# Two transformer blocks on one core: the opening's vector loads, its scales and its order of turning rearranged

## The reference, cut to what matters

```python
h = jnp.concatenate([meta, x], axis=1)          # 16 meta tokens + 256 tokens, width 2048
u = rms_norm(h, norm_mix_pre[i])                # xf * rsqrt(mean(xf * xf) + eps) * g
u = conformer_conv(u, conv_w_in[j], ...)        # begins with u @ w_in + b_in, w_in 2048 x 4096
...                                             # layer norm, swiglu, then the second block with its experts
```

## Time and profile before

| | us |
|---|---|
| median of three timed runs (2286.61 to 2288.72) | 2287.68 |
| span of the profiled execution | 2283.6 |
| TensorE busy in it | 2254.0 |
| VectorE, ScalarE, GpSimd busy | 1607.3, 1208.3, 248.0 |

### The profile page before, as it was taken

The page is one execution under the profiler, slowest core; times in us unless marked ns, Lnnn a source line. Parts: engine busy times, 40 slices in busy tenths (PEclk is TensorE's granted clock), DMA queues, the critical chain, the costliest instruction groups (busy, mean ns, idle before and its releaser), DMA issues.

```text
span 2283.6 us, 34678 instructions
## 1 busy us (share of the span) xinstructions
PE 2254.0 (99%) x12099; PEld 1943.3 (85%) x12099; DVE 1607.3 (70%) x1910; ACT 1208.3 (53%) x1229; POOL 248.0 (11%) x107
## 2 busy tenths in 40 slices
PE   9999999999999999999999999999999999999997
PEld 8999788888888888888888888888887888888886
DVE  2999776565556554545587665567558898999997
ACT  4445456444444444344553454444356778787785
POOL 4898101000000000000100000000010000101000
PEclk9999999999999999999999999999999999999999
DMA  7665256776676665555577666655566999999995
GB/s 202 177 177 175 104 195 167 192 188 184 189 191 189 184 191 183 196 189 197 173 191 206 170 185 193 188 166 184 185 239 238 385 370 365 375 369 391 370 378 229
DMA packets 446150, 514.93 MB, mean 225 GB/s; under 512 B 12911, under 2 KB 407847, under 8 KB 410279
## 3 DMA queue, kind: packets, MB, share of 16 engines
q1 hardware_dynamic: 443268, 502.21, 67.6%
q0 software_dynamic: 2544, 11.66, 1.3%
q10 hardware_dynamic: 272, 0.20, 0.0%
HBM read 512.36 MB, written 6.29 MB: 227 GB/s over the span
## 4 chain that ended last, share of the span: by engine, by line
PE 92%; DVE 3%; issue 2%; ACT 2%; POOL 1%; DVEq 0%; ACTq 0%; POOLq 0%
PE ps L2438 25%; PE ps L2332 16%; PE ps L2443 13%; PE ps L2647 10%; PE ps L2664 7%; PE ps L2652 5%; PE ps L2512 2%; PE ps L2251 2%; PE ps L2233 2%; PE ps L2234 2%; ACT whi L726 1%; DVE ps L1385 1%; PE ps L2345 1%; POOL wlo L556 1%; PE ps L2174 1%
## 5 line engine op out<-in xcount | busy, mean ns | idle before, releaser
L726 ACT ACTIVATE whi<-raw 128x2048 fp32r<-128x2048 f32 x286 | 547.4, 1914 | 359.6 <-PE ps L2332 184.8
L1305 DVE TENSOR_TENSOR wlo<-raw,whi 128x2048 fp32r<-128x2048 f32 x248 | 567.8, 2289 | 205.4 <-ACT whi L726 205.4
L2438 PE MATMUL ps<-xT,whi 128*128 128x512 f32 x2656 | 638.9, 392 | 5.3 <-DVE xT L1749 4.3
L2438 PEld LDWEIGHTS ps<-xT,whi 128*128 128x128 f32 x2656 | 488.5, 189 | 99.8 <-issue 4.4
L2443 PEld LDWEIGHTS ps<-xT,wlo 128*128 128x128 f32 x2656 | 343.5, 192 | 14.3
L2443 PE MATMUL ps<-xT,wlo 128*128 128x256 f32 x2656 | 347.8, 283 | 0.0
L990 ACT ACTIVATE wk<-ps 128x256 f32<-128x256 f32 x184 | 68.8, 383 | 450.4 <-PE ps L2443 450.1
L2332 PE MATMUL ps<-whi,act 128*128 128x512 f32 x1088 | 259.5, 391 | 0.0
L2332 PEld LDWEIGHTS ps<-whi,act 128*128 128x128 f32 x1088 | 205.4, 189 | 43.6 <-ACT act L908 0.9
L1311 DVE TENSOR_TENSOR wlo<-raw,whi 128x2048 fp32r<-128x2048 f32 x94 | 214.2, 2288 | 3.9 <-ACT whi L736 3.5
L736 ACT ACTIVATE whi<-raw 128x2048 fp32r<-128x2048 f32 x88 | 168.1, 1914 | 32.2 <-PE ps L2647 23.1
(11 more groups left out here) (339 smaller groups left out, 2704.9 us busy)
## 6 DMA issues: line engine op xcount, KB each, us to landing
raw<-in_w_in SPq DMA_DIRECT2D x72, 1024.0 KB, 5.5
raw<-in_w_exp_up SPq DMA_DIRECT2D x56, 1024.0 KB, 7.4
raw<-in_ffn_w_gate SPq DMA_DIRECT2D x44, 1024.0 KB, 5.6
raw<-in_ffn_w_up SPq DMA_DIRECT2D x44, 1024.0 KB, 5.6
raw<-in_ffn_w_down SPq DMA_DIRECT2D x44, 1024.0 KB, 4.8
raw<-in_w_exp_gate SPq DMA_DIRECT2D x40, 1024.0 KB, 6.4
raw<-in_conv_w_in SPq DMA_DIRECT2D x32, 1024.0 KB, 6.0
more_raw<-in_w_exp_down SPq DMA_DIRECT2D x32, 1024.0 KB, 7.9
```

Source lines behind the costliest of these rows:

```text
L726: fn(whi[:, s % 2, :], raw[:, s % RING, :], ACT.Copy).then_inc(hi_ready, 1)
L1305: V.tensor_tensor(wlo[:, s % 2, :], raw[:, s % RING, :], whi[:, s % 2, :], ALU.subtract).then_inc(lo_ready, 1)
L2438: mm(ps[:, bank, :], whi[:, s % 2, at:at + P], xT5[:, k0 + k, :], start=(k == 0), stop=False)
```

## The change

The seven vector loads are issued by GpSimd in place of ScalarE. ScalarE squares and sums the meta tokens itself, takes their root, then square and root of token half 0, then of half 1, each root on its own; VectorE makes a reciprocal and a diagonal after each. TensorE multiplies ones 8 times, turns the meta tokens unscaled into bank 6 (16 transposes), multiplies ones 8 times, and makes a broadcast of the meta tokens' scales by a product of ones and `meta_d`. It turns half 0 for k = 0 to 7 as soon as its diagonal is there, two k to a bank, then the vectors, then half 1 for the same k. VectorE multiplies all turned meta tokens at once by the gain and by the scale (`metaF`), ScalarE copies them to `xTA` at k = 2, and VectorE makes their residue in one instruction. Evictions and residues take the 256 token columns alone. ScalarE makes the high part of panel 0 at k = 4 and of panel 1 at k = 8. TensorE's products begin at k = 12 of the turning, and after it k = 4 to 15 of panel 0 run with k = 0 to 7 of panel 1, followed by low products, the other eight k of panel 1 and its low products. In the diff, the declarations of six semaphores are left out.

```diff
--- before.py
+++ after.py
@@ -234,6 +234,7 @@
 
         x_d = tmp[:, 0, 0:T].rearrange("p (t c) -> p t c", t=TOK)
         meta_d = tmp[0:META, 0, T:T + META]
+        metaF = tmp[:, 0, 2 * T:2 * T + KT * META].rearrange("p (k c) -> p k c", k=KT)
 
         FIRST_ROWS, FIRST_TURN = (4, 5, 6, 7), (3, 1, 2, 4)
         OHG = TOK * (GROUPS + EXPERTS) + 2 + 2 * 4 * TOK
...
@@ -545,9 +552,14 @@
             pool.affine_select(out=ident[:, :], in_=ident[:, :], compare_op=ALU.not_equal, fill=1.0, base=0,
                                pattern=[[-1, P]], channel_multiplier=1).then_inc(ident_ready, 1)
 
+            for src, at in ((norm_mix_pre, V_PRE), (conv_b_in, V_BIN), (conv_b_dw, V_BDW), (conv_ln_g, V_LG),
+                            (conv_ln_b, V_LB), (norm_ffn_pre, V_FPRE), (norm_mix_g_2, V_MIX2)):
+                r = src.rearrange("a (k p) -> (a k) p", p=P)
+                pool.dma_start(vst[at:at + r.shape[0], 0, :], r).then_inc(vec_first, 16)
+
             pool.wait_ge(ssq_ready, 2)
             pool.memset(uext[:, :, 0:PAD], 0.0).then_inc(pad_ready, 1)
-            pool.wait_ge(meta_sq, 2)
+            pool.wait_ge(meta_sq, 1)
             pool.memset(sq_acc, 0.0).then_inc(acc_clear, 1)
 
             def panel_lo(g, s):
@@ -749,29 +761,35 @@
 
 
             a.dma_start(gB[0:META, :], meta_tokens).then_inc(meta_in, 16)
-            for src, at in ((norm_mix_pre, V_PRE), (conv_b_in, V_BIN), (conv_b_dw, V_BDW), (conv_ln_g, V_LG),
-                            (conv_ln_b, V_LB), (norm_ffn_pre, V_FPRE), (norm_mix_g_2, V_MIX2)):
-                r = src.rearrange("a (k p) -> (a k) p", p=P)
-                a.dma_start(vst[at:at + r.shape[0], 0, :], r).then_inc(vec_first, 16)
-
             a.wait_ge(var_ready, 3)
             warm(2)
-            for t in range(TOK):
-                a.wait_ge(x_in[t], 16)
-                squares(h[:, t, :], t)
+            a.wait_ge(meta_in, 16)
+            fn(tmp[0:META, 1, :], gB[0:META, :], ACT.Square, accum_out=st[0:META, SS + 2:SS + 3]).then_inc(meta_sq, 1)
+            a.wait_ge(meta_sq, 1)
+            fn(st[0:META, RT + 2:RT + 3], st[0:META, SS + 2:SS + 3], ACT.Sqrt, bias=st[0:META, EPS_AT:EPS_AT + 1],
+               scale=1.0 / D).then_inc(open_root, 1)
+            a.wait_ge(x_in[0], 16)
+            squares(h[:, 0, :], 0)
+            a.wait_ge(ssq_ready, 1)
+            fn(st[:, RT:RT + 1], st[:, SS:SS + 1], ACT.Sqrt, bias=st[:, EPS_AT:EPS_AT + 1],
+               scale=1.0 / D).then_inc(open_root, 1)
+            a.wait_ge(x_in[1], 16)
+            squares(h[:, 1, :], 1)
             a.wait_ge(ssq_ready, 2)
-            a.wait_ge(meta_sq, 2)
-            root(st[:, SS:SS + 3], st[:, RT:RT + 3], 1.0 / D, st[:, EPS_AT:EPS_AT + 1])
+            root(st[:, SS + 1:SS + 2], st[:, RT + 1:RT + 2], 1.0 / D, st[:, EPS_AT:EPS_AT + 1])
 
 
             a.wait_ge(vec_ready, 1)
             for k in range(KT):
                 if k == 2:
+                    a.wait_ge(meta_scaled, 2)
+                    fn(xTA[:, :, 0:META], metaF, ACT.Copy).then_inc(meta_hi, 1)
+                if k == 4:
                     hi(0, 0)
-                if k == 10:
+                if k == 8:
                     hi(0, 1)
-                a.wait_ge(turned, k + 1)
-                fn(xTA[:, k, 0:TM], ps[:, k % 4, 0:TM], ACT.Copy,
+                a.wait_ge(turned, k // 2 * 2 + 2)
+                fn(xTA[:, k, META:TM], ps[:, k // 2 % 4, k % 2 * T:k % 2 * T + T], ACT.Copy,
                    scale=vcol[:, V_PRE + k:V_PRE + k + 1]).then_inc(xhi_ready, 1)
 
 
@@ -1322,24 +1340,39 @@
             V.memset(st[:, EPS_AT:EPS_AT + 1], RMS_EPS).then_inc(var_ready, 1)
             V.memset(st[:, LN_EPS_AT:LN_EPS_AT + 1], LN_EPS).then_inc(var_ready, 1)
 
-            v.wait_ge(var_ready, 1)
-            v.wait_ge(meta_in, 16)
-            V.tensor_tensor(tmp[0:META, 1, :], gB[0:META, :], gB[0:META, :], ALU.mult).then_inc(meta_sq, 1)
-            v.wait_ge(meta_sq, 1)
-            V.reduce_sum(st[0:META, SS + 2:SS + 3], tmp[0:META, 1, :], AX_X).then_inc(meta_sq, 1)
+            v.wait_ge(ident_ready, 1)
+            v.wait_ge(open_root, 1)
+            V.reciprocal(st[0:META, RS + 2:RS + 3], st[0:META, RT + 2:RT + 3]).then_inc(scale_ready, 1)
+            v.wait_ge(scale_ready, 1)
+            V.tensor_scalar(meta_d, ident[0:META, 0:META], st[0:META, RS + 2:RS + 3], None, ALU.mult).then_inc(scale_ready, 1)
+            v.wait_ge(open_root, 2)
+            V.reciprocal(st[:, RS:RS + 1], st[:, RT:RT + 1]).then_inc(scale_ready, 1)
+            v.wait_ge(scale_ready, 3)
+            V.tensor_scalar(x_d[:, 0, :], ident[:, :], st[:, RS:RS + 1], None, ALU.mult).then_inc(scale_ready, 1)
+            v.wait_ge(root_ready, 1)
+            V.reciprocal(st[:, RS + 1:RS + 2], st[:, RT + 1:RT + 2]).then_inc(scale_ready, 1)
+            v.wait_ge(scale_ready, 5)
+            V.tensor_scalar(x_d[:, 1, :], ident[:, :], st[:, RS + 1:RS + 2], None, ALU.mult).then_inc(scale_ready, 1)
             v.wait_ge(vec_turned, 1)
             V.tensor_copy(vT[:, 0, :], ps[:, 7, 0:P]).then_inc(vec_ready, 1)
-            v.wait_ge(root_ready, 1)
-            V.reciprocal(st[:, RS:RS + 3], st[:, RT:RT + 3]).then_inc(scale_ready, 1)
-            v.wait_ge(scale_ready, 1)
-            V.tensor_scalar(meta_d, ident[0:META, 0:META], st[0:META, RS + 2:RS + 3], None, ALU.mult).then_inc(scale_ready, 1)
-            for t in range(TOK):
-                V.tensor_scalar(x_d[:, t, :], ident[:, :], st[:, RS + t:RS + t + 1], None, ALU.mult).then_inc(scale_ready, 1)
+            v.wait_ge(vec_ready, 1)
+            v.wait_ge(meta_turned, 1)
+            v.wait_ge(meta_rs, 1)
+            V.tensor_tensor(metaF, ps[:, 6, 0:KT * META].rearrange("p (k c) -> p k c", k=KT),
+                            vcol[:, V_PRE:V_PRE + KT].rearrange("p (k a) -> p k a", a=1).to_broadcast([P, KT, META]),
+                            ALU.mult).then_inc(meta_scaled, 1)
+            v.wait_ge(meta_scaled, 1)
+            V.tensor_tensor(metaF, metaF,
+                            ps[:, 6, T:T + META].rearrange("p (a c) -> p a c", a=1).to_broadcast([P, KT, META]),
+                            ALU.mult).then_inc(meta_scaled, 1)
             for k in range(KT):
-
-                v.wait_ge(xhi_ready, k + 1)
-                V.scalar_tensor_tensor(out=xTA[:, k, TM:2 * TM], in0=ps[:, k % 4, 0:TM],
-                                       scalar=vcol[:, V_PRE + k:V_PRE + k + 1], in1=xTA[:, k, 0:TM],
+                if k == 2:
+                    v.wait_ge(meta_hi, 1)
+                    V.tensor_tensor(xTA[:, :, TM:TM + META], metaF, xTA[:, :, 0:META], ALU.subtract).then_inc(meta_lo, 1)
+
+                v.wait_ge(xhi_ready, k // 2 * 2 + 2)
+                V.scalar_tensor_tensor(out=xTA[:, k, TM + META:2 * TM], in0=ps[:, k // 2 % 4, k % 2 * T:k % 2 * T + T],
+                                       scalar=vcol[:, V_PRE + k:V_PRE + k + 1], in1=xTA[:, k, META:TM],
                                        op0=ALU.mult, op1=ALU.subtract).then_inc(xlo_ready, 1)
             v.wait_ge(vec_turned, 2)
             V.tensor_copy(flat(vT[:, 1:5, :])[:, 0:TAPS * KT], ps[:, 7, 0:TAPS * KT])
@@ -2173,12 +2206,29 @@
                 for _ in range(count):
                     mm(ps[:, bank, 0:P], ones[:, :], ones[:, :], start=True, stop=True)
 
-            keep_busy(46, 6)
+            keep_busy(8, 5)
+            pe.wait_ge(meta_in, 16)
+            for k in range(KT):
+                i = tr(ps[:, 6, k * META:(k + 1) * META], gB[0:META, k * P:(k + 1) * P], ident[0:META, 0:META])
+            i.then_inc(meta_turned, 1)
+            keep_busy(8, 5)
+            pe.wait_ge(scale_ready, 2)
+            mm(ps[:, 6, T:T + META], ones[0:META, :], meta_d, start=True, stop=True).then_inc(meta_rs, 1)
+
+            def turn_first(k, t):
+                at = k % 2 * T + t * P
+                return mm(ps[:, k // 2 % 4, at:at + P], h[:, t, k * P:(k + 1) * P], x_d[:, t, :], start=True, stop=True)
+
+            pe.wait_ge(x_in[0], 16)
+            pe.wait_ge(scale_ready, 4)
+            for k in range(KT // 2):
+                turn_first(k, 0)
             pe.wait_ge(vec_first, 16 * 7)
             tr(ps[:, 7, 0:P], vst[:, 0, :], ident[:, :]).then_inc(vec_turned, 1)
-            pe.wait_ge(x_in[0], 16)
             pe.wait_ge(x_in[1], 16)
-            keep_busy(8, 6)
+            pe.wait_ge(scale_ready, 6)
+            for k in range(KT // 2):
+                turn_first(k, 1).then_inc(turned, 1)
 
             def hi_products(k, slot):
                 w = whi[:, slot, k * P:(k + 1) * P]
@@ -2194,30 +2244,24 @@
 
 
 
-            LAG = 4
-            pe.wait_ge(vec_ready, 1)
-            for k in range(KT):
-                if k >= 4:
-
-                    pe.wait_ge(xlo_ready, k - 3)
-                if k == 0:
-                    pe.wait_ge(scale_ready, 4)
-                b = ps[:, k % 4, :]
-                mm(b[:, 0:META], gB[0:META, k * P:(k + 1) * P], meta_d, start=True, stop=True)
```

(24 more changed lines are left out.)

## The result

The changed kernel takes 2275.97 us (median; four runs, 2275.41 to 2280.22) beside 2287.14 of the kernel before on the same chip: ratio 0.9949, 95% interval 0.9936 to 0.9963. It is faster, as forecast, by 11.2 us between the medians where 9.3 were forecast. The profiled execution spans 2273.6 us, its own time is 2275.52, so 1.9 us lie around the span. The span is 10.0 shorter than before's 2283.6.

A forecast was written before the change was run, and what follows sets the result against it. TensorE, busy 99% of the span, bounds the kernel, and time is lost in its opening. Opening's end 43.16 to 33.4 gives 9.7, less 0.4 for handovers: 2287.7 - 9.3 = 2278.4 us, own range 2276 to 2280, wider 2275.5 to 2284.0.

The forecast's parts named there:

- the gain doesn't pass through: Rival: the convolution stage starts on a date of its own, so the time stays at 2287; chance 0.07.
- the 0.4 for handovers: Opening: 0.4 us taken off the gain for some eight more semaphore handovers, bounds 0 to 0.8.
- Half 1's root: Opening, ScalarE: root does not move, as ScalarE is free when half 1 lands at 9.7; cost 0 to 0.1 us.
- The ones: Opening, TensorE: second eight matmuls of ones take 1.8 us, ending at 8.9, before half 0's turnings at 10.2.
- clock rival: Opening: fewer ones and TensorE half idle from 14 to 19 drop the clock; gain only 4.5 to 8; chance 0.22.
- The work from k = 12: Opening, TensorE: from 19.2, remaining turnings, products and low products sum to 14.2 us, end at 33.4 against 43.16.
- The vector loads: Rival: loads on GpSimd's queue land after 12.5, each microsecond later costing one; chance 0.08 at 13 to 16, 0.05 very late.
- the median of the timed runs is 4.1 above that, and I carry a difference over unchanged: Whole kernel: profiled span 2283.6 us, median 4.1 above; the forecast gain is subtracted from 2287.7.
- 2 us either way: Behind the opening: allowance for low-clock stretches shifting against the work when all comes 9 us earlier.
- the wider range: Whole time 2275.5 to 2284.0: gain from 12.2 (no handover cost, 2 us more later) to 3.7 (clock rival's dear end, late vectors).
- late vectors: Opening: vector loads landing at the upper bound of 15.2 leave a gain of 6.6 (2281.1); vectors at 13 to 16, chance 0.08.

The follow-up runs named there:

- the added products: Changed kernel with one more 16-row product per k in half 1's turning loop, its result unused; 2297.43 us in its one execution.
- the last two experiments: Eight one-row bias products behind the convolution made 128-row: changed kernel, bias left out, 2273.21 us; bias kept, with GpSimd's high part and 16 and 4 ones, 2271.83 us.
- the refilled gap: Kernel before with 30 matmuls of ones ahead of the vectors' turn in place of 46, and 10 behind it in place of 8; 2287.79 us, 0.9992.

## Where the prediction held, and the step that failed

**Where the gain lies: right.** Work that starts earlier in the opening passes through whole: 9.56 us at the opening's end, 10.0 in the span, between two executions with the same 10.2 us at the lower level behind the convolution. The rival that the gain doesn't pass through falls.

**The steps, forecast and measured** (us of the span):

| step | forecast | after |
|---|---|---|
| meta tokens' root there | 7.35 | 7.7 |
| half 1's squares start | 9.7 | 10.10 |
| half 0's turnings | 10.2 | 11.74 |
| last vector load landed | 12.2 (11.4 to 15.2) | 10.9 |
| vectors' turn | 12 to 12.5 | 13.63 |
| half 1's diagonal ready | 12.6 | 12.99 |
| first eviction | 13.3 | 14.45 |
| high part of panel 0 | 15.5 | 16.21 |
| turning of k = 12 | 19.2 | 19.82 |
| opening's end (chain) | 33.4, with the 0.4 for handovers 33.8 | 33.60 |

*Half 1's root* moved by 0.4 although ScalarE was free: half 1 landed some 8.8 us after its issue (at about 10.1) in place of before's 8.4 (9.7). Over the other openings this time lies between 8.1 and 9.0, with before's order of loads between 8.4 and 8.7, so much of it is spread between executions; a share of the change in it is not shown. *The ones* were priced at 1.8 us for the second eight, the higher level; they took 3.78 at the lower one, so half 0 came 1.5 late. That is a piece of the clock rival, in a place where the rival had not put it, and it is a matter of the execution: in the execution of this opening shown beside the added products, the same 16 records took 2.05 and half 0 turned at 10.59, near the forecast. Of those 1.5 us 1.1 were left at the first eviction and 0.6 at k = 12, since what follows hangs on evictions. *The work from k = 12* took 13.8 where the sum had 14.2: its first four k took 2.9, not 3.3, since the forecast kept the 0.64 us for the token turnings of one k, which take 0.44 where no product of 16 rows stands between them. So the end is right within 0.2, by errors of opposite sign. Nothing new was late behind it: the low products (L2241) follow without a wait for GpSimd, and in the chain VectorE's copy of the vectors at 34.84 is followed by the next panels' products at 35.08, with no wait for a transfer.

**The clock rival: did not come true behind 12 us, but its mechanism is real.** After's clock is 1.00 from 16 to 20 us, with TensorE busy 2.71 of 4, and the durations (0.71 for the token turnings of one k, as before) say the same:

```profile
16.00:20.00 4.00, 2.71 (x19) 2.34 (x20) 2.43 (x7) 4.00 (x7) 1.80 (x1) 1.00 1.02 259
```

The rule that stood for it, the Trainium skill, "TensorE: Matmul & The Clock Gate", section "HAM oscillation — how this bites in real kernels", is borne out elsewhere: an idle time of 2.11, 3.67, 4.12 or 5.97 us brought a low clock behind it in the four variants that had one, for 3.4 to 23.9 us. The change's own idle times, 0.56 and 1.03 us, did not. The example in that section of the Trainium skill has waits longer than the bursts between them. Here the bursts (1.95 us and more) are the longer, so the forecast read the rule too widely when it said that the rival would come true by it. The price was undersized: 8 us later than before with fewer ones alone, where I allowed a loss of 1.4 to 4.9.

**The vector loads: right side, the bound too dear.** By the list of transfers they landed 5.9 to 6.5 us after issue, the last at 10.9, and were not waited for. Their price when late is about 1:1, as the rival had it. That GpSimd's queue frees ScalarE is worth 0.5 to 0.9 us, in a kernel whose ScalarE has taken over the meta tokens' squares.

**The step that failed: "the median of the timed runs is 4.1 above that, and I carry a difference over unchanged".** In every run with a profile the time of the profiled execution is 1.7 to 1.9 us above its span. So the profiled execution of before stood for a time of 2285.3 to 2285.5, not for the median of 2287.68: it was one of its shortest (2285.0 to 2293.0 over all runs). The 4.1 held 2.2 us of another thing, and the forecast added them to a span that did not have them. By its own span the sum is 2283.6 - 9.3 + 1.9 = 2276.2, against 2275.97 measured. The 2.4 us by which the forecast was off are these 2.2, 0.7 of the span (10.0 where 9.3 were forecast), less 0.45 by which the median of after lies above its profiled execution.

What the 2.2 us were is, by the clocks, a second term that was mis-sized, *"2 us either way" for stretches at the low clock later on*. Behind the opening's end the span holds 2240.2 to 2241.9 us in the five profiles with 10 to 14 us at the lower level behind the convolution (before, after, half 0 held back, the loads late, fewer ones alone), and 2245.6 to 2247.8 in the seven with 20 to 24 (the others but the last two experiments): 5 to 6 us, whatever the edit in the opening. No trace of a longer execution of before exists, but the mean clocks agree: of the 52 executions of before that ran beside the variants, the 21 with a mean granted clock of 0.989 or 0.990 took 2290.37 to 2293.01 us, and the 31 with 0.991 or 0.992 took 2285.03 to 2289.52. That term alone is as large as half the gain. It moves the comparison of medians between 8.8 and 11.2, and so, as far as the runs show, it is chance on which side of the range 2276 to 2280 a median of the change falls: 2275.97 the first time, 2281.28 the second. Between the shortest executions of both kernels (2285.0 of 56 and 2275.4 of 9) the gain is 9.6, that of the opening.

The ends of the wider range, 2275.5 to 2284.0, don't follow from the terms given for them. No handover cost and 2 us more are a gain of 9.7 + 2 = 11.7, not 12.2, or 2276.0; the dear end of the clock rival (4.5) with late vectors (2.7 less) is 1.8, not 3.7, or 2285.9. That 2275.97 lies inside it rests on that slip.

**Where the 9.6 us come from.** The two traces account for all of it. From the turning that is not done ahead (half 1 in the change) to the opening's end, before and after, columns as the earlier trace rows:

```profile
15.73:43.00 27.27, 27.27 (x193) 24.71 (x193) 7.73 (x16) 12.77 (x19) 11.86 (x3) 1.00 0.71 187
```

```profile
13.74:33.44 19.70, 18.10 (x147) 17.54 (x146) 8.02 (x20) 11.76 (x20) 10.94 (x3) 1.00 1.11 284
```

The stretch starts 2.0 earlier and is 7.6 shorter. TensorE is busy 9.2 less in it and waits 1.6, where before it never waited. The panels' products are the same 96 records, so the 9.2 lie in the turning: 1.9 for half 0's first eight, done ahead; 5.1 for the meta columns (16 times 0.32); and 2.2 that remain, for token turnings that are quicker with no product of 16 rows between them, as in the chain of after beside the 0.64 of the earlier trace rows:

```profile
20.78 0.44 PE ps L2220 x4
```

2.0 + 1.9 + 5.1 + 2.2 - 1.6 = 9.6. This is a sum over rows, of which experiments bear out parts: the start by the refilled gap (1.9), half 0 ahead by holding it back (1.3, and 2.9 with the clock), and the price of the meta columns on TensorE by their return to the loop (0.74 in place of 0.24 for a k, until the clock fell). No run took the meta columns' share of the opening apart at a steady clock.

**Open.** Why the clock stays low behind the convolution for 10 us in one execution and 20 in another of the same kernel: the runs show that the products of one row bring it, not what decides the length. Nor do they show why the opening of the changed kernel reaches the higher level before 6.7 us in one execution and at 11 or later in others.

## What to carry to other kernels

Ones that keep TensorE busy are no free filler: take them out only together with the gap that they fill, for the gap can cost more at a low clock (8 us here) than the ones did (2 us). A small product between large ones can cost more than its own time: here 0.32 us itself and 0.2 for its neighbours. Before a sum is made against a median, put the profiled execution's own time beside it, and look for a stretch whose granted clock differs between executions; its spread belongs in the range. When an instruction is moved to GpSimd, look at what VectorE reads from SBUF at the same time.

## What was not expected of the hardware

- Products of a single row, with TensorE busy 32 of 32 us, stood in a stretch with a granted clock of 0.63 to 0.84; with 128 rows in their place it was 0.95, and executions came within 1.5 to 2.5 us of one another instead of 8.
- In two variants the opening's loop, with its products of 16 rows, stayed at 1.2 GHz for 23.9 us though TensorE was busy all that time; in the three that fell without such products it came back after 3.4 to 6.8 us.
- Two token records of 128 x 128 took 0.42 us behind a product of 16 rows and 0.24 without one, both at the higher level.
- A VectorE instruction of 0.41 us took 4.57 beside one GpSimd instruction of 4.6 that began 0.2 earlier.
- The same opening rises to the higher level at about 11.6 us in one execution, at about 11 in another and before 6.7 in a third (16 records of ones in 3.78, 3.67 and 2.05 us).
